# Two-layer streaming encoder: in-projection groups 7 to 15 in seven products for the second token half, with weight parts stored in the first

## What is computed

```
for l in range(DEPTH):                              # 2
    h = rmsnorm(x, norm_gain[l])
    q, k, v, g_attn, x_rnn, g_rnn = split(h @ w_in[l])          # 2048 x 4352
    attn = sliding_window_attention(q, k, v, sinks[l], rope)    # window 128, chunks of 64
    rnn = rg_lru(causal_conv(x_rnn, conv_w[l]), gates...)
    x = x + concat(attn * silu(g_attn), rnn * silu(g_rnn)) @ w_out[l]   # 2048 x 2048
return rmsnorm(x, final_gain)
```

## Time and profile before

| | us |
|---|---|
| median of 3 runs | 2313.31 (2311.88 to 2314.69) |
| profiled execution, its own time | 2315.93 |
| its span in the trace | 2313.4 |
| PE busy | 2295.0 |
| DVE busy | 1568.3 |
| ACT busy | 1345.1 |

### The profile page before, as it was taken

The page is one execution under the profiler, slowest core; times in us unless marked ns, Lnnn a source line. Parts: engine busy times, 40 slices in busy tenths (PEclk is TensorE's granted clock), DMA queues, the critical chain, the costliest instruction groups (busy, mean ns, idle before and its releaser), DMA issues. The chain is left out here.

```text
span 2313.4 us, 36679 instructions
## 1 busy us (share of the span) xinstructions
PE 2295.0 (99%) x13798; PEld 1921.3 (83%) x13798; DVE 1568.3 (68%) x2548; ACT 1345.1 (58%) x2566; POOL 32.2 (1%) x58
## 2 busy tenths in 40 slices
PE   9998999999999999999999999999999999999999
PEld 8886888899888888889888888888988888888898
DVE  7566877755556877866676687785565478778555
ACT  7556766444455866645565676763454557666444
POOL 1110000000000000000000000000000000000000
PEclk9999999999999999999999999999999999999999
DMA  8887333344333233344435433333443333333444
GB/s 267 238 251 220 90 90 91 107 135 137 94 104 92 85 93 90 88 145 142 154 114 157 149 128 94 89 96 110 141 126 98 92 94 88 92 89 99 119 134 155
DMA packets 139665, 288.04 MB, mean 125 GB/s; under 512 B 16224, under 2 KB 20576, under 8 KB 136800
## 3 DMA queue, kind: packets, MB, share of 16 engines
q1 hardware_dynamic: 136368, 260.44, 37.4%
q0 software_dynamic: 2688, 25.17, 4.5%
q10 hardware_dynamic: 432, 0.10, 0.0%
HBM read 277.25 MB, written 33.55 MB: 134 GB/s over the span
## 5 line engine op out<-in xcount | busy, mean ns | idle before, releaser
L606 PE MATMUL proj<-operand,wcut 128*128 128x512 f32 x8376 | 1947.4, 391 | 3.0 <-DVE x L1517 3.0
L606 PEld LDWEIGHTS proj<-operand,wcut 128*128 128x128 f32 x8376 | 1565.2, 188 | 340.3 <-issue 11.0
L831 ACT ACTIVATE wcut<-wraw 128x512 fp32r<-128x512 f32 x872 | 549.7, 630 | 852.6 <-PE proj L606 716.8
L1230 DVE TENSOR_TENSOR wcut<-wraw,wcut 128x512 fp32r<-128x512 f32 x873 | 601.9, 689 | 641.2 <-ACT wcut L831 637.6
L626 PE MATMUL proj<-xsum_out,wcut 128*128 128x256 f32 x1104 | 140.4, 283 | 0.0
L626 PEld LDWEIGHTS proj<-xsum_out,wcut 128*128 128x128 f32 x1104 | 137.9, 192 | 2.4
L626 PE MATMUL proj<-operand,wcut 128*128 128x256 f32 x828 | 106.7, 283 | 0.0
L626 PEld LDWEIGHTS proj<-operand,wcut 128*128 128x128 f32 x828 | 104.3, 192 | 2.1
L989 ACT ACTIVATE prob<-ps_at,stat 128x128 f32<-128x128 f32 x256 | 90.1, 363 | 0.8
L937 ACT ACTIVATE gy<-proj 32x512 f32<-32x512 f32 x144 | 85.0, 590 | 3.8
L1517 DVE TENSOR_TENSOR x<-proj,x 128x512 f32<-128x512 f32 x62 | 39.9, 686 | 30.1 <-PE proj L606 30.1
(11 more groups left out here) (173 smaller groups left out, 1500.7 us busy)
## 6 DMA issues: line engine op xcount, KB each, us to landing
wraw<-in_w SPq DMA_DIRECT2D x712, 256.0 KB, 2.6
wraw<-weight_sums SPq DMA_DIRECT2D x92, 256.0 KB, 2.6
weight_sums<-in_blocks POOLq DMA_DIRECT2D x36, 512.0 KB, 6.6
wraw<-in_blocks SPq DMA_DIRECT2D x69, 256.0 KB, 2.6
x<-in_xt SPq DMA_DIRECT2D x2, 4096.0 KB, 16.3
mixed<-in_xt SPq DMA_DIRECT2D x14, 512.0 KB, 6.8
weight_sums<-weight_sums POOLq DMA_DIRECT2D x12, 512.0 KB, 5.1
gw<-in_gates SPq DMA_DIRECT2D x32, 128.0 KB, 2.7
```

What stands on the lines that cost most here:

```text
L606: last = pe.matmul(bank_of(l, 2 * g + m)[:, :], wcut[:, n % RING, a, c:c + P], operand[:, k, b, :], start=(k == 0 and i == 0), stop=(k == ...
L831: act.activation(wcut[:, u % RING, 0, :], wraw[:, u % RING, :], ACT.Copy).then_inc(w_hi, 1)
L1230: dve.tensor_tensor(wcut[:, u % RING, 1, :], wraw[:, u % RING, :], wcut[:, u % RING, 0, :].bitcast(F32), ALU.subtract).then_inc(w_lo, 1)
```

## The change

It does these things together:

- Groups 7 to 15 of the in-projection join the seven products, in the second token half alone, in both layers (`IN_SEVEN`): 18 groups.
- In the first token half these groups take four of their units as 2 x 2 blocks ("block" units) with whole columns, so that the blocks' high and low parts come to stand in `wcut`. Seven of the eight units of each group are stored from there to memory (`weight_cuts`), high and low part together, 512 KB a unit; the eighth block isn't used in the seven products. In the second half those seven are loaded ready-made into `wcut` (`READY`), without ACT and DVE; the four block sums of a group are loaded from `weight_sums` and split as before. A group in seven products has 11 units.
- POOL's queue builds the block sums of these groups too, behind those of the out-projection: 16 batches instead of six (two of them with one group).
- The ring has six places. `wraw` is gone: the raw unit lands in the place of the low part, and the low part is written over it. So a unit's place can be loaded only when PE is done with it (`unit_done`) and, where it was stored, when the store has landed (`cut_out`).
- The operand sums of the in-projection lie in the room of `x`. In the second half's layer 1, x is therefore stored to memory at slots 1 to 4 (4 MB) and loaded again from slot 127 on. In layer 0 the 4 MB load of x at slot 60 becomes eight loads of 512 KB from slot 127 on, in both halves.
- In a seven-product group followed by another, the third late unit comes after the next group's lead units, not before.
- Eight of the operand tiles of layer 1 are split in slots 0 to 3 instead of the last slots of layer 0, and conv's odd tiles in the second half move from 6 slots after their group to 2.

```diff
-RING = 4
-AHEAD = RING - 1
+RING = 6
+AHEAD = 3
+IN_LAST = 15
+IN_SEVEN = {(0, 0): (), (0, 1): (), (1, 0): range(7, IN_LAST + 1), (1, 1): range(7, IN_LAST + 1)}
+SEVEN = {(h, l): (*IN_SEVEN[h, l], *range(PG + 2, PG + (7 if (h, l) == (LAST, DEPTH - 1) else 8)))
...
     if mine and ahead:
-        return [t[:2], p[:1], p[1:2], t[2:], a[:2], a[2:], p[2:3], p[3:]]
+        return [t[:2], p[:1], p[1:2], p[2:3], a[:2], a[2:], t[2:], p[3:]]
...
+BATCH.sort(key=lambda batch: batch[1] < PG)
+KEYS = []
+CUT_AT = {}
+for n, (h, l, kind, g, j) in enumerate(UNIT):
+    if h == 0 and zone_of(g) == "in" and g in BUILT[l] and (kind, j) != ("block", WHOLE[A21]):
+        CUT_AT[key_of(l, kind, g, j)] = n
+        KEYS.append(key_of(l, kind, g, j))
+READY = {n for n, (h, l, *unit) in enumerate(UNIT) if h > 0 and key_of(l, *unit) in CUT_AT}
...
-        wraw = sb("wraw", [RING, KU * GW])
         wcut = sb("wcut", [RING, 2, KU * GW], F32R)
+        wall = over("wall", nc.sbuf_base - 4 * RING * 2 * KU * GW, [RING, 2, KU * GW], F32)
...
+            def w_load(n):
+
+                at = n if n < TOTAL else n - UPG
+                h, l, kind, g, j = UNIT[at]
+                what = {"lead": LEAD, "late": LATE_OF}[kind][j][0] if kind in ("lead", "late") else None
+                if what in SUMS:
+                    sp_.wait_ge(built[what], 32 * (batch_of(l, g) + 1))
+                if n in READY:
+                    from_n = CUT_AT[key_of(l, kind, g, j)]
+                    sp_.wait_ge(cut_out[from_n % RING], 16 * stores_through(from_n))
+                    sp_.dma_start(wcut[:, n % RING, :, :].rearrange("p a c -> p (a c)").bitcast(F32),
+                                  cuts[KEYS.index(key_of(l, kind, g, j))]).then_inc(w_in[n % RING], 16)
+                    return
+                sp_.dma_start(wall[:, n % RING, 1, :], source(at)).then_inc(w_in[n % RING], 16)
...
-                            sp_.wait_ge(w_lo, u + 1)
-                            if h == 0 and what in SUMS:
-                                sp_.wait_ge(built[what], 32 * (batch_of(UNIT[next_u][1], g) + 1))
-                            sp_.dma_start(wraw[:, u % RING, :], source(next_u)).then_inc(w_in[u % RING], 16)
+                            if u + RING < TOTAL:
+
+                                sp_.wait_ge(unit_done, u + 1)
+                                if u in STORED:
+                                    sp_.wait_ge(cut_out[u % RING], 16 * stores_through(u))
+                                w_load(u + RING)
+                            if u + 2 in STORED:
+
+                                sp_.wait_ge(w_lo, SPLIT_NO[u + 2])
+                                sp_.dma_start(cuts[KEYS.index(key_of(l, *UNIT[u + 2][2:]))],
+                                              wcut[:, (u + 2) % RING, :, :].rearrange("p a c -> p (a c)").bitcast(F32)
+                                              ).then_inc(cut_out[(u + 2) % RING], 16)
...
+                if n in READY:
+                    pe.wait_ge(w_in[n % RING], 16 * (n // RING + 1))
+                else:
+                    pe.wait_ge(w_lo, SPLIT_NO[n])
...
                 act.wait_ge(w_in[u % RING], 16 * (u // RING + 1))
-                if u >= TOTAL:
-                    act.wait_ge(unit_done, u + 1)
-                elif u >= RING:
-                    act.wait_ge(unit_done, u - RING + 1)
```

More of the change, by code:

```diff
@@ L158 @@
 VT_TR = 18
-Q_EV = 16
+Q_AT = [2 * UPG + 4 * t for t in range(AT)]
 NB = NCH * NKV
@@ L172 @@
 T_AT = {(h, l, "out"): (126, 128, 136, 143) for h in range(HALVES) for l in range(DEPTH)}
+T_AT.update({(1, 0, "in"): (25, 33, 41, 49), (1, 1, "in"): (6, 7, 9, 11)})
 T_ORDER = {(h, l, "out"): (0, 1, 2, 3) for h in range(HALVES) for l in range(DEPTH)}
-HI_PART = {"out": (0, 0, 0, 0)}
+T_ORDER.update({(h, l, "in"): ((2, 0, 3, 1), (0, 1, 2, 3))[l] for h in range(HALVES) for l in range(DEPTH)})
+T_ROOM = (1, 3, 0, 2)
+HI_PART = {"in": (0, 0, 0, 1), "out": (0, 0, 0, 0)}
+SPILL = (1, 3, 0, 2)
+SPILL_AT = 1
+RELOAD = UPG * IN_LAST + 7
 START_SUMS = 8
@@ L275, in build @@
         x_in = [sem(f"x_in{i}") for i in range(KT // 2 + 1)]
-        xres_in = sem("xres_in")
+        xres_in = [sem(f"xres_in{i}") for i in range(KT // 2)]
         tab_in = sem("tab_in")
@@ L279, in build @@
         built = {n: sem(f"built{n}") for n in SUMS}
+        cut_out = [sem(f"cut_out{i}") for i in range(RING)]
+        kept = [sem(f"kept{i}") for i in range(4)]
+        stored = [sem(f"stored{i}") for i in range(4)]
         unit_done = sem("unit_done")
@@ L498, in _ @@
                                 x_load(h + 1, i)
+            for n in range(TOTAL, TOTAL + UPG - RING):
+                sp_.wait_ge(unit_done, n + 1)
+                w_load(n)
             for a, b in STORES_A:
@@ L596, in whole @@
                 h, l, kind, g, j = UNIT[n]
-                for kk in range(KU):
-                    k = KU * j + kk
-                    if g in (0, PG):
-                        pe.wait_ge(op_lo, at_op(h, l, g // PG, k))
[L601 to L608, removed]
+                if kind == "plain":
+                    parts = [(KU * j + kk, m, kk * GW + m * P) for kk in range(KU) for m in range(2)]
+                else:
+                    parts = [(KU * pair + j % 2, j // 2, P * i) for i, pair in enumerate(JS[zone_of(g)])]
+                for k, m, c in parts:
+                    if g in (0, PG) and m == 0:
+                        pe.wait_ge(op_lo, at_op(h, l, g // PG, k))
+                    for i, (a, b) in enumerate(((0, 0), (0, 1), (1, 0))):
+                        if (k, m, c) == parts[-1] and i == 2 and n + 1 < TOTAL:
+                            next_bank(n + 1)
+                        last = pe.matmul(bank_of(l, 2 * g + m)[:, :], wcut[:, n % RING, a, c:c + P],
+                                         operand[:, k, b, :],
+                                         start=(i == 0 and k == 0),
+                                         stop=(k == KT - 1 and i == 2), skip_group_check=g in SEVEN[h, l])
                 return last
@@ L643, in half_unit @@
                         for n, (a, b) in enumerate(((0, 0), (0, 1), (1, 0))):
-                            last = pe.matmul(last_bank(half, m)[:, 0:HT], wcut[:, (TOTAL + j) % RING, a, c:c + P],
+                            last = pe.matmul(last_bank(half, m)[:, 0:HT], wcut[:, slot, a, c:c + P],
                                              operand[:, k, b, HT * half:HT * half + HT],
@@ L1113, in _ @@
                                 square(h, 1, k)
-                            for k in (KT - 2, KT - 1):
+                        for k in range(X_EARLY, KT):
+                            if l == 1 and s == (k - X_EARLY) // 2:
                                 x_hi(h, 1, k)
```

180 lines of the change are left out of this document (123 added, 57 removed).

## The result

The changed kernel takes 2375.95 us in the median of 4 runs (2374.13 to 2383.3), the kernel before 2314.0 us beside it: a ratio of 1.0273, 95% interval 1.0258 to 1.0287. It is slower, as forecast, but by 62 us where 13 were forecast, and outside the range. The traced execution of the changed kernel is the slowest of the four, 2383.3 us, and that of the kernel before took 2315.93 us; so the stage differences read from the traces add up to 68 us where the medians differ by 62.

What follows compares the result with a forecast made beforehand. The prediction took PE's own matmul time and its few standstills as the bound. It summed 2315.9 - 15.9 - 10.9 + 36 + 1 + 3 = 2329 us, as a median 2326.5 us, range 2290 to 2355 us.

Steps and rivals of the forecast that it cites:

- A: Rival: transfers bind groups 7 to 15 of layer 0, first half; 2326.5 us, 2316 to 2353; chance 0.42.
- Stores and sums in layer 0: First half, groups 7 to 15: SP's loads and stores compete with POOL's chain for the engines; plus 36 us.
- I take 51%, between them: 29.0 us a group: SP's queue's assumed engine share in groups 7 to 15 of layer 0; 4.5 us more a group, 41 us.
- the ring's credit: The six-place ring, full when the layer 0 store stage begins, gives back some 5 us of 41.
- C: Rival: PE standstills beside the chain's batches lower the clock; about 20 us more, 2347 us; chance 0.15.
- Seven products: Half-width matmuls replace whole units in 18 second-half in-projection groups; 0.88 us less a group, 15.9 us in all.
- combining the lead products: Extra DVE sums and ACT copies between lead and late units of 18 groups; plus 3 us.
- fewer splits in the second half gain nothing by themselves: Weight preparation by ACT and DVE runs ahead of PE, so dropping splits there saves no time.
- The load of x: Moving layer 0's 4 MB load from slot 60 removes PE's standstill and slow matmuls; minus 10.9 us in all.
- D: Rival: DVE comes late to lead sums, 18 groups lose 1 us or more each; 2341 or 2313 us; chance 0.08.
- E: Rival: HBM limit of about 358 GB/s holds, nine groups lose over 300 us; about 2610 us; chance 0.02.
- B: Rival: POOL's chain gives way, batches stretching to 40 us, SP's queue losing nothing; 2290 us, middle 2298; chance 0.33.

Runs made afterwards that it cites:

- the kernel with the chain later: Changed kernel, but POOL's queue starts the ten in-projection batches only after PE has finished slot 136 of layer 0; 2314.53 us, ratio 1.0003.
- the kernel with the ring alone: Changed kernel without any in-projection group in seven products, so no stores or further batches; six-place ring, late x load and moved units kept; 2302.72 us, ratio 0.9959.

## Why the prediction was wrong

**Right: the sign, the place, the mechanism.** The loss is where A put it, 87.7 of the 97.6 us in groups 7 to 15 of layer 0, and nearly all of it needs stores and chain together; layer 1's stores cost nothing; no loss in the out-projection; start, operand sums and x to memory and back are within 2 us.

**Wrong: the term "Stores and sums in layer 0", 36 us, which measured 97.6 us** (some 90 us in the median execution, by the estimate above). The step that failed is "I take 51%, between them: 29.0 us a group". A group took 87.7/9 = 9.7 us more than the 24.4 us it should, some 34 us; the other 9.9 us are in slots 128 to 136, where the sum had nothing. SP's queue got 46.0%, just under the 46.9% that the earlier trace rows had shown and that I held for the lower end, and moved its bytes at 42.86 MB in 46.0% of 253 us, 368 GB/s, where the sum took the 400 GB/s of the earlier trace rows: 46.0% of 34 us is 15.7 us of all engines a group, not 14.8. Behind it stands a premise, that SP's queue always has work waiting. It hasn't: a load may be issued only when the store from its place has landed. I looked at this for layer 1 ("A store is issued two units (5.5 us) before its place is wanted") with a landing of 4.9 us, and left it out for layer 0, although gave loads of half the size 5.0 us in the median and 11.7 at most beside the chain. The landing of stores from 200 to 473 us, in the changed kernel and, without the chain, from 305 to 418 us in the kernel with the chain later:

```profile
DMA to landing us min/median/max: 3.9/8.5/14.1
```

```profile
DMA to landing us min/median/max: 3.7/3.9/6.4
```

8.5 us is more than 5.5, 3.9 less. At the measured pace of 34 us a group two units last 8.5 us, just the landing's median. The experiment with the earlier store gives the landing one unit more; then the queue gets 52.7%, and the nine groups lose 39.7 us, where my sum said 41 before the ring's credit. So the sum came out about right for full engines, and what it lacked is the held place, 52 us in the traced executions; what a still earlier store would give no run shows. The ring's credit of 5 us shows at most in the first group, which lost 6.2 us, 3.5 less than the mean.

**C was a part of it, at nothing in the sum.** PE stood for 66 us of the stretch (I had 25 to 60), and its busy time was 272 us against 241 us, since the clock was at its lower level for part of it (0.83 to 0.91 in the mean). So 31 of the 97.6 us are slower matmuls, where the rival had priced 20 and the sum nothing, and where I had argued that the queue catches up meanwhile. How much the lower clock itself cost can't be told from these runs, since standstills bring it and a slower PE gives the transfers time.

**Seven products: 15.9 us forecast, some 16 measured.** The table's rows of the second half's two layers give 9.0 us and 10.0 us. But against the kernel with the ring alone, which has the same moved operand tiles and the same ring, each of the two layers gained 8.1 us. So the term is right, and of the 3 us put against it for combining the lead products nothing shows. But "fewer splits in the second half gain nothing by themselves" was true only of the kernel before: with the seven products and raw units 9.5 us of a layer's gain went.

**The load of x: 10.9 us forecast, 10.9 us in its stretch and 9 us in the median** when moved alone.

**D** played no part in the changed kernel: PE is busy in all of 1410 to 1637 us. **E** neither: from 200 to 453 us SP's queue moved 42.86 MB and the chain read and wrote 29.45 MB, 402 GB/s together, more than E allows. Nor **B**: the chain did stretch, from the 26.5 us of the earlier trace rows to 33 to 36 us a batch, but not to 40.

## What to carry to other kernels

Before adding a transfer to a buffer ring, write down for each place the whole cycle (load, landing, split, use, store, landing) and compare it with the ring's length at the landing times of a busy stretch, not of a quiet one; a queue that must wait for landings doesn't get the share that arithmetic on bytes gives it. When two streams of transfers together ask for more than the engines have and one of them isn't urgent, give it its own stretches of the program: two waits in POOL's queue were worth 78 us here (2375.95 to 2297.53 us). A fixed program order on ScalarE carries a late load to work that doesn't need it. And take a loss that is to be taken off a median from an execution near the median: here the traced one was 7 us above it, and two forecasts missed by some of that.

## What was not expected of the hardware

The shares of two queues added to 95% while SP's queue waited for landings, and to 100% with one store more in flight, at 314 GB/s instead of 287. Stores of 512 KB landed after 3.9 us in the median alone and after 8.5 us beside the chain. Cutting the chain's rows to a quarter slowed its batches from 33 to 36 us to 41 to 47 us and gave SP's queue only 2.5 points of share, although the long rows had taken 81.5% against 16.8% in the earlier trace rows.
